# Differential mixer of a streaming encoder step on one Trainium2 core: values in column halves, the root in rows, the combination ahead of the maxima, and small fills of the last mixer moved

## The reference

```python
def diff_block(q, q_pos, k, v, k_pos, t5_table, lam):
    qf = q.astype(F32).reshape(*q.shape[:3], 2, C_QK_DIM)       # two halves of 32
    kf = k.astype(F32).reshape(*k.shape[:3], 2, C_QK_DIM)
    s = jnp.einsum('bqhmd,bkhmd->bmhqk', qf, kf) * C_QK_DIM ** -0.5
    ...
    p = jax.nn.softmax(jnp.where(mask, s + bias, -jnp.inf), axis=-1)
    w = p[:, 0] - lam * p[:, 1]
    return jnp.einsum('bhqk,bkhd->bqhd', w, v.astype(F32))
...
oc = rms_norm(oc, p['c_subln_g'][l]) * (1.0 - lam_init)         # per head, over its 64 values
```

## Time and profile before

| | us |
|---|---|
| median of 3 runs | 1499.99 |
| lowest, highest | 1498.17, 1503.12 |
| the profiled execution | 1497.65 |
| its span (first to last instruction) | 1495.9 |
| TensorE busy in it | 1448.4 |
| VectorE, ScalarE, GpSimd busy | 690.1, 417.5, 272.6 |
| C: first scores to first scores of D | 224.1 to 413.0 |
| D, then B: first scores | 413.0, 550.4 |

### The profile page before, as it was taken

One profiled execution on the slowest core, in us unless ns is written; L12 is line 12 of the kernel. 1 busy time (PEld: TensorE's weight loads), 2 busy tenths in 40 slices (PEclk: granted clock), 3 DMA queues, 4 the chain that ended last, 5 costly groups with the idle time before them and its releaser, 6 DMA issues.

```text
span 1495.9 us, 23065 instructions
## 1 busy us (share of the span) xinstructions
PE 1448.4 (97%) x8862; PEld 1281.2 (86%) x8862; DVE 690.1 (46%) x1267; ACT 417.5 (28%) x1036; POOL 272.6 (18%) x428
## 2 busy tenths in 40 slices
PE   5999999999999989999999999999999999999997
PEld 4988887777878867778989899999999998989895
DVE  6335754666625345445452525344444434352516
ACT  4223445554546666533101010101000000101013
POOL 6224654433422112225000000000000000000002
PEclk9999999999999999999999999999999999999998
DMA  5321102100021123010411101011111111100003
GB/s 177 112 71 47 29 16 75 42 17 15 15 75 33 35 70 123 19 54 6 136 57 29 56 28 56 28 56 42 42 46 40 55 55 29 56 28 28 0 0 134
DMA packets 90481, 75.91 MB, mean 51 GB/s; under 512 B 5672, under 2 KB 83017, under 8 KB 90397
## 3 DMA queue, kind: packets, MB, share of 16 engines
q1 hardware_dynamic: 90412, 75.00, 16.4%
HBM read 64.06 MB, written 10.77 MB: 50 GB/s over the span
## 4 chain that ended last, share of the span: by engine, by line
PE 91%; DVE 3%; ACT 2%; POOL 1%; issue 1%; DMA 1%; SPq 0%; DVEq 0%; POOLq 0%; ACTq 0%
PE acc L794 25%; PE acc L796 24%; PE acc L795 24%; PE acc L941 5%; PE acc L965 3%; PE acc L1003 3%; PE acc L987 2%; PE acc L809 1%; PE acc L1111 1%; DVE low_z L1433 1%; DMA x_in<-in_x_prompt_dram 1%; DVE acc L1436 1%; PE acc L860 0%; PE acc L879 0%; DVE prob_slot L1457 0%
## 5 line engine op out<-in xcount | busy, mean ns | idle before, releaser
L794 PE MATMUL acc<-ohi,gu_hi 128*128 128x384 f32 (+1 forms) x1056 | 345.0, 327 | 1.8 <-issue 1.8
L796 PE MATMUL acc<-ohi,gu_lo 128*128 128x384 f32 (+1 forms) x1056 | 344.9, 327 | 0.0
L795 PE MATMUL acc<-olo,gu_hi 128*128 128x384 f32 (+1 forms) x1056 | 344.6, 326 | 0.0
L1313 ACT ACTIVATE silu<-acc 128x384 f32<-128x384 f32 (+1 forms) x66 | 31.2, 473 | 640.1 <-PE acc L796 640.1
L794 PEld LDWEIGHTS acc<-ohi,gu_hi 128*128 128x128 f32 x1056 | 198.8, 188 | 2.7 <-issue 2.2
L795 PEld LDWEIGHTS acc<-olo,gu_hi 128*128 128x128 f32 x1056 | 198.9, 188 | 0.4
L796 PEld LDWEIGHTS acc<-ohi,gu_lo 128*128 128x128 f32 x1056 | 198.8, 188 | 0.0
L1570 DVE TENSOR_TENSOR prod<-acc,silu 128x384 f32<-128x384 f32 (+1 forms) x66 | 35.4, 536 | 338.2 <-ACT silu L1313 338.2
L1590 DVE TENSOR_TENSOR x<-acc,x 128x512 f32<-128x512 f32 x198 | 134.5, 689 | 69.1 <-PE acc L796 64.4
L1640 POOL TENSOR_SCALAR meansq<-sumsq 128x1 f32<-128x1 f32 (+1 forms) x27 | 9.5, 352 | 802.8 <-ACT sq_junk L1139 770.6
L794 PE MATMUL acc<-xhi,win_hi 128*128 128x384 f32 (+1 forms) x384 | 132.1, 344 | 6.7 <-POOL xlo L1649 3.6
(11 more groups left out here) (206 smaller groups left out, 2436.9 us busy)
## 6 DMA issues: line engine op xcount, KB each, us to landing
win_raw<-in_w_in_dram SPq DMA_DIRECT2D x22, 512.0 KB, 3.9
gu_raw<-in_w_gate_dram SPq DMA_DIRECT2D x22, 512.0 KB, 3.9
gu_raw<-in_w_up_dram SPq DMA_DIRECT2D x22, 512.0 KB, 4.7
down_raw<-in_w_down_dram SPq DMA_DIRECT2D x22, 512.0 KB, 3.9
x_in<-in_x_prompt_dram SPq DMA_DIRECT2D x8, 512.0 KB, 6.9
wo_raw<-in_w_out_dram SPq DMA_DIRECT2D x8, 512.0 KB, 4.4
x<-in_x_prompt_dram SPq DMA_DIRECT2D x8, 512.0 KB, 4.7
out_dram<-y_out SPq DMA_DIRECT2D x8, 512.0 KB, 2.6
```

Source lines behind the costliest of these rows:

```text
L794: pe.matmul(out, a_hi, b_hi, start=first, stop=False)
L795: pe.matmul(out, a_hi, b_lo, start=False, stop=False)
L796: return pe.matmul(out, a_lo, b_hi, start=False, stop=last)
L1313: act.activation(silu[:, q % 2, 0:n], bank(2 * (q % 2), n), ACT.Silu).then_inc(silu_done, 1)
```

## The change

Six parts:

1. C's values are taken for two heads at once, in the column-half form (`values_turned`), in every second round (`valued_at`: 21, 23, ... 55). `values`, `turn_out`, `o_rows` and its copy go.
2. The root of the mean square comes one round later (`rooted_at`: 22, 24, ... 56). ScalarE squares the 128 partitions of both heads (`c_square`, at the end of the round before); TensorE multiplies the squares by a two-column matrix of 1/64 (`mean_square`, after the scores and the fills of place 0), so the mean stands with frames on partitions; VectorE adds epsilon times the squared row sum and copies the result scaled by the gain (`add_epsilon`); GpSimd takes the power and spreads it over 64 columns a head (`root_of_mean`); TensorE turns that (`turn_factor`, after the fills of place 1); VectorE multiplies (`output_normal`, after the maxima). GpSimd makes epsilon times the squared row sum for each head behind `inverse_sums`.
3. `combine` of r-1 stands ahead of the maxima of r where its width is 384 or more (tiles 2 to 7), behind them elsewhere.
4. `room` counts 0.22 instead of 0.33 us a block for C, which moves fills of C's rounds. By the planner's arithmetic rounds 35, 39, 43 and 48 then have a whole projection, 46 one of 320 columns in one place, and 28 and 32 only a `rows` fill in place 0.
5. Fills of B: D's rounds but the last take the projections; the three `vr` fills go from 71 to 72 (places 0, 1, 2) and the two `rows` fills of B from 69 and 70 to 73 (places 0 and 1).
6. The output products go one round later (74 to 91), the split of w_out tile 4 from 71 to 72 (and that of tile 0 from 67 to 66, with its weight slot), and the load of x1 of tiles 0 and 1 from SP's iteration 73 to 78. The gain of C is loaded as a column, twice.

```diff
-    own = w / 600 + job.blocks * (0.33 if job.mixer == "C" else 0.43)
+    own = w / 600 + job.blocks * (0.22 if job.mixer == "C" else 0.43)
...
-           *cached("B"), *mixed(values_by_columns("B"), [*rows("B", (7,), (8,)), *values_turned("B", (0, 1, 2))]),
-           *values_turned("B", (3, 4, 5), (6, 7, 8))], "D")
+           *cached("B"), *values_by_columns("B")], "D", slice(17))
+    stand([*values_turned("B", (0, 1, 2), (3, 4, 5), (6, 7, 8)), *rows("B", (7,), (8,))], "DB", slice(17, 20))
...
+    def valued_at(r):
+        us = units_at(r - V_LAG)
+        if us and units[us[0]][0].mixer == "C":
+            return [us[0] - 1, us[0]] if units[us[0]][0].head % 2 else []
+        return us
+    def rooted_at(r):
+        us = units_at(r - V_LAG - 1)
+        return valued_at(r - 1) if us and units[us[0]][0].mixer == "C" else []
...
-        OUT_SPOT = [(B0 + 1 + k, 1) for k in range(18)]
+        OUT_SPOT = [(B0 + 2 + k, 1) for k in range(18)]
...
                     load_x1(range(6, NT))
+                if r == B0 + 6:
                     sp.wait_ge(o_split, 14)
                     load_x1(range(2))
...
-            def turn_out(u):
-                job = units[u][0]
-                n = batches[("o", u)]
-                pe.wait_ge(out_done, outs[u])
-                wait_batch(pe, n - 2)
-                for t in range(2):
-                    mm = pe.transpose(bank(4 + n % 2, job.rows, at=t * P),
-                                      o_rows[0:job.rows, (u // 4) % 2, t * P:(t + 1) * P],
-                                      ident[0:job.rows, 0:job.rows])
-                mm.then_inc(batch_ready, 1)
+            def mean_square(us):
+                n = units[us[0]][0].rows
+                k = (us[0] - first_c) // 2
+                if k == 0:
+                    pe.wait_ge(part_ready, 4)
+                pe.wait_ge(c_squared, k + 1)
+                pe.matmul(bank(6, 2, n, P), c_sq[:, 0:n], sum_part[:], start=True, stop=True).then_inc(c_mean, 1)
+            def turn_factor(us):
+                n = units[us[0]][0].rows
+                pe.wait_ge(c_spread, (us[0] - first_c) // 2 + 1)
+                pe.wait_ge(c_scaled, (us[0] - first_c) // 2 + 1)
+                pe.matmul(bank(6, n, P, 2 * P), c_factor[0:n], ident[0:n, 0:n], start=True, stop=True).then_inc(c_turned, 1)
...
                 for part in parts_at(r, 0):
                     fill(*part)
-                us = units_at(r - V_LAG)
-                if len(us) == 1:
-                    values(us[0])
-                elif us:
-                    values_turned(us)
+                if rooted_at(r):
+                    mean_square(rooted_at(r))
+                elif valued_at(r):
+                    values_turned(valued_at(r))
                 for part in parts_at(r, 1):
                     fill(*part)
+                if rooted_at(r):
+                    turn_factor(rooted_at(r))
+                    if valued_at(r):
+                        values_turned(valued_at(r))
                 for k in out_at(r):
                     out_first(k)
-                if block_at(r - O_LAG) is not None:
-                    turn_out(block_at(r - O_LAG))
                 for u in units_at(r - T_LAG):
                     turn_probs(u, 0)
                 for part in parts_at(r, 2):
...
-            def c_square(u):
-                job, k = units[u][0], u - first_c
-                n = job.rows
-                act.wait_ge(pv_done, u + 1)
-                act.wait_ge(inv_ready, inv_count[u])
+            def c_square(us):
+                n, k = units[us[0]][0].rows, (us[0] - first_c) // 2
+                act.wait_ge(pv_done, us[1] + 1)
                 if k:
-                    act.wait_ge(c_factor, k)
-                act.activation(c_junk[0:n], bank(6, 64, n, 64 * (u % 2)), ACT.Square,
-                               scale=row_inv[0:n, job.n:job.n + 1], accum_out=c_var[0:n, 1:2]).then_inc(cvar_sum, 1)
+                    act.wait_ge(c_mean, k)
+                act.activation(c_sq[:, 0:n], bank(6, n), ACT.Square).then_inc(c_squared, 1)
...
+            def soon(u):
+                return units[u][0].width >= 384
...
+            def add_epsilon(us):
+                n, k = units[us[0]][0].rows, (us[0] - first_c) // 2
+                dve.wait_ge(c_mean, k + 1)
+                dve.wait_ge(eps_ready, us[1] - first_c + 2)
+                if k:
+                    dve.wait_ge(c_rooted, k)
+                dve.tensor_tensor(c_mean_sq[0:n, 0:2], bank(6, 2, n, P),
+                                  eps_sum[0:n, us[0] - first_c:us[1] - first_c + 1], ALU.add).then_inc(c_added, 1)
+                if k:
+                    dve.wait_ge(out_done, outs[us[0] - 1])
+                dve.tensor_scalar(c_out[:, 0:n], bank(6, n), subln[:, 0:1], None, ALU.mult).then_inc(c_scaled, 1)
+            def output_normal(us):
+                job, n, k = units[us[0]][0], units[us[0]][0].rows, (us[0] - first_c) // 2
+                dve.wait_ge(c_turned, k + 1)
+                dve.wait_ge(c_scaled, k + 1)
+                dve.tensor_tensor(qT["C"][:, job.q_tile, job.q_col:job.q_col + n], c_out[:, 0:n], bank(6, n, P, 2 * P),
+                                  ALU.mult).then_inc(out_done, 1)
...
+                for u in units_at(r - 1):
+                    if units[u][0].mixer == "C" and soon(u):
+                        combine(u)
+                if rooted_at(r):
+                    add_epsilon(rooted_at(r))
                 if r < NR and pairs[r][0].mixer != "A":
                     for job in pairs[r]:
                         maximum(job)
                 for u in units_at(r - 1):
-                    if units[u][0].mixer == "C":
+                    if units[u][0].mixer == "C" and not soon(u):
                         combine(u)
-                us = units_at(r - V_LAG)
-                if len(us) == 1:
-                    output(us[0])
-                elif us:
+                if rooted_at(r):
+                    output_normal(rooted_at(r))
+                us = valued_at(r)
+                if us and units[us[0]][0].mixer != "C":
...
+                if a.mixer == "C":
+                    k = u - first_c
+                    pool.tensor_scalar(eps_sum[0:n, k:k + 1], eps_col[0:n], row_sum[0:n, a.n:a.n + 1],
+                                       row_sum[0:n, a.n:a.n + 1], ALU.mult, ALU.mult).then_inc(eps_ready, 1)
+            def root_of_mean(us):
+                n, k = units[us[0]][0].rows, (us[0] - first_c) // 2
+                pool.wait_ge(c_added, k + 1)
+                pool.tensor_tensor(c_mean_sq[0:n, 2:4], c_mean_sq[0:n, 0:2], minus_half[0:n, 0:2], ALU.pow)\
+                    .then_inc(c_rooted, 1)
+                pool.wait_ge(c_rooted, k + 1)
+                if k:
+                    pool.wait_ge(c_turned, k)
+                both = c_mean_sq[0:n, 2:4].rearrange("p (h o) -> p h o", o=1).to_broadcast([n, 2, 64])
+                pool.tensor_tensor(c_factor[0:n].rearrange("p (h n) -> p h n", h=2),
+                                   ones[0:n].rearrange("p (h n) -> p h n", h=2), both, ALU.mult).then_inc(c_spread, 1)
```

## The result

The changed kernel takes **1521.37 us** (median, 1520.37 to 1522.89) beside 1499.87 of the kernel before: ratio 1.0142, 95% interval 1.0122 to 1.0161. Slower, as forecast (1512.5), but beyond the range of 1497 to 1519. The profiled execution took 1520.37, span 1518.6, so 22.7 above that of before.

What follows compares the result with a forecast made beforehand. TensorE was taken as the bound, with a VectorE-GpSimd loop setting C's tiles 2 to 7 after the change. C +2, moved fills +11.4 and output +0.5 gave +13.9, 1511.6 profiled; median forecast 1512.5 us, range 1497 to 1519.

Steps and rivals of the forecast that it cites:

- Values in column halves, -15.6, and the root's two products, +8.6: TensorE work in C: taking values for two heads at once saves 15.6 us; mean of squares and factor turn add 8.6.
- +0.45 on the loop per root round: VectorE in every second round of C: epsilon sum and scaled copy ahead of the maxima add 0.45 us (0.3 to 0.7).
- The loop of 2R + exp + combination + 2.48: C, tiles 2 to 7: maxima, exponential, inverse, combination form a loop without TensorE; R is the first reduction; 137.8 us with root steps.
- The rounds with more TensorE work than the loop, +7.0: C rounds 29, 35, 39, 43, 45, 48, 49: TensorE's work, with whole projections in some, outlasts the loop, adding 7.0 us.
- Rounds 28 and 32: C rounds with only a rows fill: the factor's turn waits 1.4 us each for GpSimd, mostly covered by the loop.
- Tiles 0, 1 and 8: C tiles without the new order: saved work counts, less 0.6 for short root rounds, giving -2.2 and -1.6 us.
- Rounds 68 and 69, -1.0: Late D rounds: B's rows fills gone and one wait of 0.46 us gone, saving 1.0 us.
- The stall, +11.4: Passage from D to B: ScalarE's rows copy waits for a store behind nine loads; +11.4 us net (+3 to +14).
- the third: Rival: the loop costs more through spread, epsilon, copy and inverse; C +6 to +9, 1519 us with the stall; chance 0.10.
- the first: Rival: TensorE bound throughout, fills cover the loop and the store passes the loads; 1484 us; chance 0.10.
- the second: Rival: the store isn't late, the stall is short or hidden; 1503 us, or 1497 with C low; chance 0.14.
- the fourth: Rival: column halves of C take as long as before; 1528 us; chance under 1 in 50.

## Why the prediction was right or wrong

- *What bounds the kernel*: right as a reading, but "a microsecond of TensorE work taken away is worth one, unless a wait takes its place" left out a third case: the wait that takes its place can also take the clock (of the 23 waits in C of 1.8 us or more, 22 had half clock behind them).
- *Values in column halves, -15.6, and the root's two products, +8.6*: right. The pair at eight blocks is in the chain with 1.90 us, and start to start the mean takes 0.24 and the turn 0.22 (0.24 taken). The turn of the rows, -2.1, is 18 x 0.11 = 2.0.

```profile
397.13 2.40 PE acc L948 x8
399.53 1.90 PE acc L996 x32
```

- *+0.45 on the loop per root round*: in its range (0.3 to 0.7), at the low end: 0.16 and 0.34, but the first reduction starts 0.32 behind the combination's end. Power and spread took 0.70 and 0.40. Groups of tiles 2 to 7 (busy us, mean ns | idle before):

```profile
L1705 POOL TENSOR_SCALAR eps_sum<-eps_col,row_sum 128x1 f32<-128x1 f32 x25 | 25.8, 1033 | 0.0
...
L1699 POOL TENSOR_SCALAR row_inv<-row_inv,row_sum,lam 128x1 f32<-128x1 f32 x25 | 8.9, 357 | 2.6
L1711 POOL TENSOR_TENSOR c_mean_sq<-c_mean_sq,minus_half 128x2 f32<-128x2 f32 x12 | 8.4, 697 | 13.8 <-DVE c_mean_sq L1466 13.6
L1717 POOL TENSOR_TENSOR c_factor<-ones,c_mean_sq 128x128 f32<-128x128 f32 x12 | 4.8, 400 | 0.9
```

- *The loop of 2R + exp + combination + 2.48*: right as long as nothing else stood in it. Tile 2 was forecast at 17.9 and took 17.85; tile 4 at 23.5 with its heavy round and took 23.52. In tiles 2 to 7 the first reduction waited for the scores in rounds 43 and 49 alone. Round 43 is in the tiles named as a sign of being wrong, but its scores ran at half clock.
- *The rounds with more TensorE work than the loop, +7.0*: this is the step that failed. It counted the work of rounds 29, 35, 39, 43, 45, 48 and 49 and took a fill of place 2 to start when TensorE gets there. It waits for the copy of place 1, which the loop pushes back behind both exponentials: 1.9, 1.9 and 0.9 in rounds 42, 48 and 39. And the sum held the clock at 1.00, where the two longer waits halved it for 10.2 us. Tiles 6 and 7 took 65.8 against 57.4, and tile 5, with round 39, 26.4 against 25.5; the copy moved ahead gave 59.05 in tiles 6 and 7, the old room took C from 200.9 to 194.8. A slip in the sum works the other way: the floors of rounds 35, 39 and 43 (5.7, 6.2, 6.7) hold the 0.45 of a root round, which these odd rounds aren't, so the term should have been 1.4 higher by its own rule.
- *Rounds 28 and 32, "of which the loop covers the most"*: right in round 28 and wrong in what followed round 32. The turn of the factor waited 1.5 and 2.1 us. Tile 2 shows that the first was covered. Behind the second came 6.8 us at half clock, which was in no term. Tile 3 took 21.4 all the same, against a forecast of 22.4 with its weight split (4 x 4.76 + 0.9 + 2.5); that is luck: the rest of the tile was forecast too long by more than the half clock cost.
- *Tiles 0, 1 and 8*: right (-1.9 and -2.4 against -2.2 and -1.6).
- *Rounds 68 and 69, -1.0*: the second step that failed, wrong in sign. It counted the rows that left and not how the projections that stay are cut; whole ones in place 1 leave the two lots of turns without work between them. The term is +2.4 for rounds 54 to 69.
- *The stall, +11.4 with the tail's 0.5 to add*: right in place, cause and size. First output product 34.92 behind the start of round 70, forecast 35.3; store issued 4.5 behind the first load (5.3), landed in 9.9 (11); TensorE's wait 13.1 ("some 14"). The Trainium skill, "DMA: Bandwidth & Descriptors", Queues, rings and completion order, says that descriptors of one issuing queue are taken in ring order on each DMA engine; the trace agrees: the 9.9 behind nine loads, and a stall that is gone when the store goes first.
- *The rivals*: of the third the size came true (C at +6 to +9, 1519 in all; measured +9.3 and 1521) by another mechanism than it named: the spread took 0.40 and not 0.85, epsilon sum and copy 0.32 and not 0.7, and the inverse's first step was above 0.70 in 4 of 25 rounds; the first is refuted (reductions behind the end of the combination in all but two rounds of tiles 2 to 7), the second too (13.1 of stall), and the fourth (1.90).

In sum: -0.6 ahead of C, +7.3 in C, +3.4 in D and -1.3 behind it are the 8.8 between the 13.9 of the forecast and the 22.7 measured in the profiled executions.

## What to carry to other kernels

Before a change of order is costed, ask of each buffer that TensorE shares what stands ahead of its release in the releasing engine's queue, and whether the new order pushes that back; here the copy of a fill behind two exponentials cost 6.8 us in two tiles, of the 9.1 of arithmetic saved in all of C, and moving that copy ahead only made other work wait. Work saved on a saturated engine becomes idle time once another chain is the floor. Here idle time in single waits of nearly 2 us halved the clock for what followed, and the same time in short waits did not; so list the longest single waits of a new order, and read the granted clock of a stretch ahead of any sum about it, over several executions. A small store that something waits for belongs ahead of bulk loads in its queue (11.4 us here). And one wait of 2.7 us, taken away by moving a single fill, won 0.33%, where the whole redesign lost 1.4%.

## What the hardware showed that was not expected

- **The clock falls in C behind single short waits.** The only wait in the 6.9 us ahead of the drop at 346.9 was 1.9 us long, and the 0.50 then lasted 6.8 us. Of 23 waits of 1.8 to 2.1 us, 22 had a drop behind them. Twelve waits of up to 1.1 us, in rounds 34 to 49, had none (1.00 over 111.22 us).
- **Half clock moves about.** From one profiled execution to the next there was 0 to 27.3 us of it in C, and tile 3, with its weight split, had some in most of them. It isn't the edits alone: executions with the same rounds of C differed by 6.8 us, and the 29 of the kernel before on one chip had mean clocks of 0.985 to 0.996 and took 1494.0 to 1502.3 us.
- **A one-column step on GpSimd at three times its price.** The epsilon sum (L1705) took 1.03 us in the mean and up to 1.40, as it stands beside VectorE's combination, while the like step L1699 took 0.34 with VectorE idle. It grows with the combination's width, 0.73 beside 384 columns and 1.40 beside 1024, and is each time 0.11 longer than the combination itself; the one with VectorE idle took 0.34. The Trainium skill, "GPSIMD Engine Reference", Specifications, has the two engines share their way to SBUF when VectorE reads two inputs there, as the combination does; the trace agrees. The inverse (L1694) grew from 0.69 to 0.98 and, in round 33, to 1.60 beside a split's subtraction.
